# The last block's expert rows stay on chip and are added by a one-hot product, with the row loads no longer waiting for that block

## The reference, cut to what matters

```python
def step(acc, blk):
    e, tok, wt = blk
    xb = h[tok]
    hb = jax.nn.silu(xb @ we_g[e]) * (xb @ we_u[e])
    return acc.at[tok].add(wt[:, None] * (hb @ we_d[e]).astype(jnp.float32)), None
...
shared = (jax.nn.silu(h @ ws_g) * (h @ ws_u)) @ ws_d
return (routed + shared.astype(jnp.float32)).astype(h.dtype)
...
x = x + gt2 * rms_norm(yf, g_ffn_post)
```

## Time and profile before

| | |
|---|---|
| median of 3 runs | 1137.02 us (1135.15 to 1137.31) |
| the profiled execution's span | 1136.7 us |
| PE busy | 1096.6 us, 96% |
| DVE, ACT, POOL busy | 462.9, 236.6, 137.3 us |
| TensorE clock granted, mean of the span | 0.993 of full speed |
| DMA | 337.17 MB, mean 297 GB/s |

### The profile page before, as it was taken

The page is one execution under the profiler, slowest core; times in us unless marked ns, Lnnn a source line. Parts: engine busy times, 40 slices in busy tenths (PEclk is TensorE's granted clock), DMA queues, the critical chain, the costliest instruction groups (busy, mean ns, idle before and its releaser), DMA issues.

```text
span 1136.7 us, 16992 instructions
## 1 busy us (share of the span) xinstructions
PE 1096.6 (96%) x6443; PEld 576.4 (51%) x6443; DVE 462.9 (41%) x1286; ACT 236.6 (21%) x516; POOL 137.3 (12%) x163
## 2 busy tenths in 40 slices
PE   6999999999999999999989999999999999999896
PEld 3456677777877545754433443443343444343232
DVE  2218541665456645842264223223233232231157
ACT  4131241222233123111101111111111111111111
POOL 0110000000020110121111112111112111121100
PEclk9999999999999999999999999999999999999999
DMA  9978742042270372899999999999999999999898
GB/s 317 308 262 297 227 79 54 21 84 56 65 260 2 138 267 82 343 354 340 414 414 400 421 406 421 419 403 385 417 409 353 418 408 385 415 398 363 311 406 342
DMA packets 80743, 337.17 MB, mean 297 GB/s; under 512 B 10756, under 2 KB 27496, under 8 KB 52366
## 3 DMA queue, kind: packets, MB, share of 16 engines
q1 hardware_dynamic: 62606, 287.32, 66.4%
q0 software_dynamic: 18048, 48.68, 11.7%
HBM read 311.30 MB, written 37.24 MB: 307 GB/s over the span
## 4 chain that ended last, share of the span: by engine, by line
PE 87%; DMA 8%; DVE 2%; ACT 1%; issue 1%; SPq 1%; DVEq 0%; POOLq 0%; ACTq 0%
PE bank L1545 27%; PE bank L1568 15%; PE bank L1241 10%; PE bank L1260 5%; DMA mem<-in_w_exp_down 4%; PE bank L1533 3%; DMA mem<-expert_out_rows 3%; PE bank L1359 3%; PE bank L1360 3%; PE bank L1154 3%; PE bank L1477 3%; PE bank L1238 3%; PE bank L1129 1%; PE bank L1556 1%; PE bank L1324 1%
## 5 line engine op out<-in xcount | busy, mean ns | idle before, releaser
L1545 PE MATMUL bank<-mem 128*32 128x512 f32 (+2 forms) x1424 | 304.5, 594 | 2.6 <-issue 1.6
L1545 PEld LDWEIGHTS bank<-mem 128*32 128x32 f32 (+2 forms) x1424 | 100.2, 126 | 159.3 <-issue 157.9
L1568 PE MATMUL bank<-mem 128*32 128x512 f32 (+2 forms) x712 | 158.6, 599 | 5.1 <-DMA mem<-in_w_exp_down 5.1
L2231 DVE COPY mem<-bank 128x512 f32<-128x512 f32 x48 | 33.2, 692 | 292.2 <-PE bank L1533 292.2
L1545 PE MATMUL bank<-x_sb,mem 128*32 128x512 f32 (+2 forms) x480 | 141.6, 594 | 1.1 <-issue 1.1
L1241 PE MATMUL bank<-hT,mem 128*128 128x288 f32 x512 | 133.3, 409 | 1.0 <-ACT mem L919 1.0
L1241 PEld LDWEIGHTS bank<-hT,mem 128*128 128x128 f32 x512 | 93.8, 190 | 25.8 <-issue 2.4
L1049 ACT ACTIVATE mem<-bank 128x256 f32<-128x256 f32 x48 | 18.5, 385 | 316.7 <-PE bank L1556 316.5
L1568 PEld LDWEIGHTS bank<-mem 128*32 128x32 f32 (+2 forms) x712 | 49.1, 126 | 63.8 <-issue 60.3
L1568 PE MATMUL bank<-hT,mem 128*32 128x512 f32 (+2 forms) x240 | 72.8, 596 | 1.1 <-ACT mem L1049 1.1
L1545 PEld LDWEIGHTS bank<-x_sb,mem 128*32 128x32 f32 (+2 forms) x480 | 43.6, 127 | 59.1 <-issue 59.1
(11 more groups left out here) (403 smaller groups left out, 1290.4 us busy)
## 6 DMA issues: line engine op xcount, KB each, us to landing
mem<-in_w_exp_gate SPq DMA_DIRECT2D x48, 1024.0 KB
mem<-in_w_exp_up SPq DMA_DIRECT2D x48, 1024.0 KB
mem<-in_w_exp_down SPq DMA_DIRECT2D x48, 1024.0 KB
mem<-in_w_ada SPq DMA_DIRECT2D x8, 2048.0 KB, 9.8
x_sb<-in_w_exp_gate SPq DMA_DIRECT2D x16, 1024.0 KB
x_sb<-in_w_exp_up SPq DMA_DIRECT2D x16, 1024.0 KB
hT<-in_w_exp_down SPq DMA_DIRECT2D x16, 1024.0 KB
mem<-in_w_in SPq DMA_DIRECT2D x7, 2048.0 KB, 14.2
```

The lines of the kernel that those rows point to most:

```text
L1545: i = mm(bank[sl, :].rearrange("p (m f) -> p m f", m=2), xT[:, j % 2, c * BLK + sl.start:c * BLK + sl.stop], wview(r)[0][:, :, c, :], star ...
L1568: i = mm(ps[4 + hf][sl, :], hhT[:, k * BLK + sl.start:k * BLK + sl.stop], wview(r)[1][:, k, hf * 512:(hf + 1) * 512], start=k == 0, stop=k ...
```

## The change

The output of block 47 is no longer put into `yo` and scattered. ACT and DVE copy it into a buffer of its own, `ylast`. When block 45 is worked on, DVE makes from the token numbers of block 47's rows (`toklast`) a matrix `spot` of 128 rows by T tokens with a one where the row belongs to the token (`last_spots`). After the shared expert's products PE multiplies `spot` by `ylast` into the same PSUM banks (`last_down`), two products of 512 columns for each of the five tiles. Into the rows of `expert_out_rows` that block 47 would have written, POOL scatters zeros (`zrow`), before the scatter of block 46. SP waits for the zeros and block 46's scatter, no longer for block 47, then loads q = 0 to 3; before q = 4 it waits for block 47's products and then loads the x rows too. The slots of `yhalf` are numbered anew, since q = 0 and 1 share slot 0 and the next two lie over slots that block 47 doesn't use. In the last turn of the loop PE puts `down(46)` after three chunks of `up(47)`, and ACT and DVE copy block 46's output before they turn to `silu(47)` and `gated(47)`. The renamed semaphores are left out here.

```diff
@@ -303,6 +304,8 @@
         bcG, e_ = carve(mem, e_, [2, D])
+        zrow, e_ = carve(mem, e_, [D])
+        spot, e_ = carve(mem, e_, [T])
         at += NT * D
@@ -339,6 +342,7 @@
         yo, at = carve(hflat, 0, [2, D])
+        ylast, _ = carve(hflat, at, [D])
         dnX, at = carve(hflat, at, [FJ, D])
@@ -427,9 +431,13 @@
-        def ycount(q):
-            return 16 * (q // NYH + 1)
+        def yslot(q):
+            return 0 if q < 2 else (q - 1) % NYH
+        def yrows_sem(q):
+            return S[f"yb{yslot(q)}"], 16 if q <= NYH + 1 else 32
@@ -626,12 +634,10 @@
                     load_dn(r, ids.pop(r))
-            sp.wait_ge(S["eup"], max(LASTB[r] for r in range(NE) if slot(r) == XSLOT) + 1)
-            sp.wait_ge(S["xgT_t"], NBK)
-            for t in range(NT):
-                sp.dma_start(x_sb[0:ROWS[t], t, :], x1_d[t * P:t * P + ROWS[t], :]).then_inc(S[f"ld_x{t}"], 16)
             nov = overflow_count(sp)
-            sp.wait_ge(S["edn"], NBK)
+            def last_block():
+                sp.wait_ge(S["edn"], NBK)
@@ -647,33 +653,43 @@
-            overflow(sp, nov, body, last=last_rows)
-            sp.wait_ge(S["xgT_a"], NBK)
-            sp.wait_ge(S["xgT_d"], NBK)
+            overflow(sp, nov, body, last_block, last_rows)
             for k in range(2):
...
+            def x1_load(t):
+                sp.dma_start(x_sb[0:ROWS[t], t, :], x1_d[t * P:t * P + ROWS[t], :]).then_inc(S[f"ld_x{t}"], 16)
...
                 at_ = (k0 - q % 2 * KPE) * D
-                sp.dma_start(yhalf[0:ROWS[t], q % NYH, at_:at_ + (k1 - k0) * D], yv[t * P:t * P + ROWS[t], k0 * D:k1 * D]).then_inc(S[s], 16)
+                sp.dma_start(yhalf[0:ROWS[t], yslot(q), at_:at_ + (k1 - k0) * D], yv[t * P:t * P + ROWS[t], k0 * D:k1 * D]).then_inc(s, 16)
             for k in range(2):
-                sp.dma_start(yhalf[k:P:2, 0, :], yv[SEQ:T, KPE * k * D:KPE * (k + 1) * D]).then_inc(S[f"yh{k}"], 16)
+                sp.dma_start(yhalf[k:P:2, 0, :], yv[SEQ:T, KPE * k * D:KPE * (k + 1) * D]).then_inc(S[f"ys{k}"], 16)
             for i, (t, _) in enumerate(COMBINE):
...
                     q = 2 * i + k
-                    if q == NYH:
+                    if q == 4:
+                        sp.wait_ge(S["xgT_a"], NBK)
+                        sp.wait_ge(S["xgT_d"], NBK)
+                        sp.wait_ge(S["eup"], NBK)
+                        sp.wait_ge(S["edn"], NBK)
+                        for u in range(NT):
+                            x1_load(COMBINE[u][0])
+                    if q == 6:
                         sp.wait_ge(S["yd_sum"], 1)
-                    elif q > NYH + 1:
+                    elif q > 6:
                         sp.wait_ge(S["yd_sum" if (q - NYH) % 2 else "yp_mm"], (q - NYH) // 2 + 1)
                     if i < LAST:
-                        y_rows(q, t, k * KPE, (k + 1) * KPE, f"yh{q % NYH}")
+                        y_rows(q, t, k * KPE, (k + 1) * KPE, yrows_sem(q)[0])
                     elif k == 0:
-                        y_rows(q, t, 0, KPE // 2, "yh7")
-                        y_rows(q, t, KPE // 2, KPE, f"yh{q % NYH}")
-            y_rows(2 * LAST + 1, t, KPE, TOPK - 2, f"yh{(2 * LAST + 1) % NYH}")
-            y_rows(2 * LAST + 1, t, TOPK - 2, TOPK - 1, "yh5")
-            y_rows(2 * LAST + 1, t, TOPK - 1, TOPK, "yh6")
+                        y_rows(q, t, 0, KPE // 2, S["y8a"])
+                        y_rows(q, t, KPE // 2, KPE, yrows_sem(q)[0])
+                    else:
+                        y_rows(q, t, KPE, TOPK - 2, yrows_sem(q)[0])
+                        y_rows(q, t, TOPK - 2, TOPK - 1, S["ys0"])
+                        y_rows(q, t, TOPK - 1, TOPK, S["ys1"])
             for i, (t, _) in enumerate(COMBINE):
@@ -764,9 +780,10 @@
             pool.memset(xg2, 0.0).then_inc(S["pch"], 1)
+            pool.memset(zrow, 0.0).then_inc(S["pch"], 1)
             pool.wait_ge(S["st_x"], 16 * NT)
             pool.memset(xg3, 0.0).then_inc(S["pch"], 1)
-            pool.wait_ge(S["pch"], 2)
+            pool.wait_ge(S["pch"], 3)
             pool.wait_ge(S["h2_st0"], 16 * ((NT + 1) // 2))
@@ -802,9 +819,12 @@
                     ahead(b + XG, (b + XG) % RQ, gbuf(b + XG, b + XG))
+                if b == NBK - 1:
+                    q = (NBK - 1) % RQ
+                    pool.indirect_dma_start(y_d[:, :], bass.IndirectOffsetOnAxis(idxs[:, q:q + 1], 0), zrow, None,
+                                            bounds_check=T * TOPK - 1, oob_is_err=False).then_inc(S[f"sct{q % 2}"], 16)
                 if b >= 1:
                     scatter(b - 1, (b - 1) % RQ)
-            scatter(NBK - 1, (NBK - 1) % RQ)
             nov = overflow_count(pool)
@@ -1050,6 +1070,9 @@
                 act.wait_ge(S["edn"], n + 1)
+                if isinstance(n, int) and n == NBK - 1:
+                    a(ylast[:, 0:512], ps[4][:, :], ACT.Copy).then_inc(S["eout_a"], 1)
+                    return
                 if not (isinstance(n, int) and n < 2):
@@ -1604,18 +1629,20 @@
                 new_gu(b)
-                if b < NBK - 1:
-                    up(b, b, pieces(b))
-                else:
-                    up(b, b, pieces(b), range(KC - 2))
+                if b == NBK - 1:
+                    up(b, b, pieces(b), range(2))
+                    hh_T(b - 1)
+                    up(b, b, pieces(b), range(2, 3))
+                    new_dn(b - 1)
+                    down(b - 1, pieces(b - 1))
+                    up(b, b, pieces(b), range(3, KC))
+                    break
+                up(b, b, pieces(b))
                 if b == 0:
...
                     hh_T(b - 1)
-                if b == NBK - 1:
-                    up(b, b, pieces(b), range(KC - 2, KC))
-                if b < NBK - 1:
-                    x_T(b + 1, b + 1)
+                x_T(b + 1, b + 1)
                 if b + XG < NBK:
@@ -1658,8 +1685,18 @@
+            def last_down(o):
+                t, kp = COMBINE[o]
+                n = ROWS[t]
+                if o == 0:
+                    pe.wait_ge(S["srt_ready"], 2)
+                for hf in range(2):
+                    mm(ps[2 * (o % 4) + hf][0:n, :], spot[:, t * P:t * P + n], ylast[:, hf * 512:(hf + 1) * 512], start=False, stop=False)
...
                 shared_down(o)
+            for o in range(4):
+                last_down(o)
             pe.wait_ge(S["yd_sum"], 1)
@@ -1668,24 +1705,26 @@
                 if o < LAST:
-                    pe.wait_ge(S[f"yh{q % NYH}"], ycount(q))
+                    pe.wait_ge(*yrows_sem(q))
                 else:
-                    pe.wait_ge(S["yh7"], 16)
+                    pe.wait_ge(S["y8a"], 16)
                 for hf in range(2):
...
                         i = mm(ps[2 * (o % 4) + hf][0:n, :], ident[0:n, 0:n],
...
+                if o == LAST - 1:
+                    last_down(LAST)
@@ -2222,9 +2261,18 @@
                 o = ps[6]
+                if isinstance(n, int) and n == NBK - 1:
+                    step(ts(toklast[:, :], o[:, 0:1], o[:, 3:4], float(OOB), ALU.add, ALU.add))
                 ts(idxg[:, q:q + 1], o[:, 0:1], o[:, 3:4], float(OOB), ALU.add, ALU.add)
...
+            def last_spots():
+                for t in range(NT):
+                    n = ROWS[t]
+                    i = ts(spot[:, t * P:t * P + n], iota[:, 0:n], float(t * P), toklast[:, 0:1], ALU.add, ALU.is_equal)
+                i.then_inc(S["srt_ready"], 1)
@@ -2270,17 +2321,22 @@
                     xT_evac(b + 1, b + 1)
+                else:
+                    out_rows(b - 1, b - 1)
                 gated(b, b)
...
                     table(b - 6)
-                if b >= 1:
+                if b == NBK - 3:
+                    last_spots()
+                if 1 <= b < NBK - 1:
                     out_rows(b - 1, b - 1)
...
             def first_blocks():
+                dve.wait_ge(S["sct1"], 16 * (NBK // 2))
                 place_more(NBK, NBK, 0)
```

More of the change, by code:

```diff
@@ L180, in build @@
         ntab = sb("ntab", [P, 1], I32)
+        toklast = sb("toklast", [P, 1])
         negoff, at = carve(cst["cos"], 0, [NO])
@@ L355, in build @@
             P_ready idx_mm idx_ready gat0 gat1 gat2 xgT_t xgT_a xgT_d eup egs ehh ehT_t ehT edn eout_a eout_d sct0 sct1
-            ld_gu0 ld_gu1 ld_gu2 ld_gu3 ld_d0 ld_d1 ld_d2 ld_d3 srt_ready srt_mm over yp_mm yh0 yh1 yh2 yh3 yh4 yh5 yh6 yh7 yd_sum yl_sum yf_rt x2_done out_st dch ach pch pool_step""".split()
+            ld_gu0 ld_gu1 ld_gu2 ld_gu3 ld_d0 ld_d1 ld_d2 ld_d3 srt_ready srt_mm over yp_mm ys0 ys1 yb0 yb1 yb2 yb3 yb4 y8a yd_sum yl_sum yf_rt x2_done out_st dch ach pch pool_step""".split()
         S = {n: sem(n) for n in names}
@@ L1676, in _ @@
                         i = mm(ps[2 * (o % 4) + hf][0:n, :], ident[0:n, 0:n],
-                               yhalf[0:n, q % NYH, k * D + hf * 512:k * D + (hf + 1) * 512], start=False, stop=o < LAST and k == kp - 1)
```

(20 more changed lines are left out.)

6 lines of the change are left out of this document (3 added, 3 removed).

## The result

| | before | changed |
|---|---|---|
| median | 1137.16 us (1135.15 to 1137.72, 4 runs) | 1148.57 us (1147.32 to 1149.94, 4 runs) |
| span of the traced execution | 1136.7 us | 1145.5 us |
| ratio | | 1.0107, 95% interval 1.0094 to 1.0119 |

The changed kernel is 11.4 us slower. The prediction had the direction, but its time was 4.7 us too low, and the result lies above its range. Time and span of the same execution are known for the changed kernel: 1147.32 and 1145.5 us, so 1.8 us lie outside the span. So the two traces differ by only 8.8 us, and stretches are compared here, not spans.

A forecast was written before the change was run, and what follows sets the result against it. PE was taken as the bound, nearly as late as the transfers: + 2.8 start + 8.6 products - 4.8 waits + 0.3 clock = + 6.9 us, span 1143.6, time 1143.9 us; 8-in-10 range 1140.5 to 1147.3.

The forecast's parts named there:

- Later start of block 47: PE in block 47: down(47) starts at 1072.8 in place of 1070.01, 2.8 us later; without the weights' wait 0.9.
- Products: PE in the combination: ten float32 last_down products, 20 records of 0.43 us, add 8.6 us that no pause covers.
- Waits for rows: PE in the combination: its waits for expert rows vanish, giving back at most 4.77 us.
- The pause: PE behind block 47: the jump over the extra blocks' code stays, 6.4 us from down(47) to a combination starting at 1079.2.
- Clock: PE at the combination's start: a first stretch at half clock costs 1.7 us in place of 1.44, 0.3 more.
- More half-clock stretches: Rival: new pauses before down(46) and down(47) bring half clock, 1.7 us per stretch; 1145.6 to 1147.3 us, chance 0.18.
- The sum: PE's last product: + 2.8 + 8.6 - 4.8 + 0.3 = + 6.9 us, at 1136.5 in place of 1129.6.
- DVE goes along: DVE's sample-tile sum comes 9.7 us later than 1093.90; DVE and PE both reach the end at 1136.4 to 1136.5.
- Transfers: Row loads start at about 1072.5 (up to 1077), not 1079.67; the stream has 8 us to spare, so PE binds.
- Zeros, memset, `spot`: Small additions on transfers, POOL and DVE: zeros could delay down weights 0 to 1.2 us, taken as 0; the rest falls in waits.

The follow-up runs named there:

- run 7: The kernel before with only the new order in the last turn of the block loop on PE, ACT and DVE: 1139.17 us, ratio 1.0018.
- run 2: The changed kernel without the ten one-hot products (last block's rows left out of the result): 1139.72 us, 7.9 less than the changed kernel.
- run 3: The changed kernel with the first row load held until TensorE is through the first tile of shared_down: 1145.92 us, ratio 1.0083.
- run 4: The changed kernel with the old order in the last turn on TensorE, ACT and DVE: 1140.53 us, ratio 1.0043.
- run 6: The kernel before without the five x row loads during block 47 (final outputs left wrong): 1135.34 us, ratio 0.9989.
- run 8: The changed kernel with the old last-turn order and each f32 one-hot product done as two bf16 products: 1140.16 us, ratio 1.0032.
- run 5: The changed kernel with the old last-turn order and the first row load held back, as well: 1142.43 us, ratio 1.0049.
- run 9: The changed kernel with old last-turn order and bf16 product pairs, x loads spread over q = 5, 6 and 7: 1141.31 us, ratio 1.0036.
- run 10: The changed kernel with old last-turn order and bf16 product pairs, x loads back in block 47 ahead of all rows: 1137.93 us, ratio 1.0008.
- run 11: The changed kernel with old last-turn order and f32 products, x loads back in block 47 ahead of all rows: 1140.77 us, ratio 1.0038.
- run 1: The changed kernel measured again, unaltered: 1147.63 us, ratio 1.0097.

## Why the prediction was wrong

**Later start of block 47: right.** From the first product of `up(47)` to that of `down(47)` were 12.49 us and are 15.22 now (1056.00 to 1071.22): + 2.73, predicted + 2.8. The wait for block 46's weights was 1.79 us, predicted 1.9. Alone in the kernel before (run 7) the order costs 2.1 us net.

**Products: right.** 1096.39 to 1103.60 and 1129.59 to 1131.31, 8.9 us, predicted 8.6. Run 2 gives 7.9 in time.

**Waits for rows: right.** None is left, 4.77 us given back. Runs 3, 4, 6 and 8 show the other side: what TensorE saves returns as a wait. The stream had room in the changed kernel only because TensorE was so late.

**The pause: here it failed.** The step reads: "The pause that follows, a jump over the extra blocks' code, stays." It was taken as a cost of the jump alone, 6.4 us from the first product of `down(47)` to the combination. The first part nearly held (6.7 us), but a second pause of 2.63 us came on top, and in the same kernel's other trace the first part was 7.6. How long TensorE stands is not a matter of the jump alone but of what the DMA engines do beside it. In the quiet runs 3, 4, 5, 6, 8 and 9 the branch took 3.4 to 3.7 us and was over when `down(47)` was (within 0.2 us, in run 3 well before), and TensorE then waited 1.19 us for a copy. Beside the x loads (before, and runs 7, 10, 11) it took 5.6 to 8.1 us and the pause was 2.62 to 4.96. Beside the row loads of the changed kernel it took 6.1 to 7.2 us, and a second pause came behind it: 3.02 + 2.63, 3.95 + 0.89, 4.09 + 2.73. The shortest and the longest branch are those of runs 4 and 7:

```profile
L488 PEldq COMPARE_BRANCH  x1: 3426/3426/3426, 1067.8 to 1067.8; - x1
L480 PEldq COMPARE_BRANCH  x1: 8051/8051/8051, 1071.3 to 1071.3; - x1
```

The prediction named the row loads' new start (1072.5, where its own terms give 1072.0; it was 1069.78) and did not ask what else is on those DMA engines at that moment. The queue was in view: the page counts instruction queues (queue, packets, MB, share of 16 engines).

```profile
q8 instruction: 54, 0.88, 0.3%
q14 instruction: 35, 0.29, 0.1%
```

Their times fit. The packets of q8, 16 KB each, near the jump start at 1073.21, 1076.64 and 1080.47 us before, and at 1075.04, 1080.54 and 1086.87 us in the changed kernel. Against the branch, the thirteen traces fall into two groups. In the six quiet ones the first packet starts 1.0 to 1.3 us after the branch does; in the seven others it starts 2.7 to 5.3 us after. In all thirteen the branch ends 2.3 to 2.9 us after that packet starts. So all that the branch takes longer lies before the packet. The second packet starts 0.7 to 1.3 us after the branch ends in ten traces. In the three whose row loads were issued before the branch (the changed kernel twice, and run 2) it comes 3.2, 3.7 and 4.4 us after, and those are the three with a second pause. In them TensorE goes on 2.2 to 2.3 us after the second packet starts. (The distance to the third packet says nothing: it was over 6 us in runs 4, 7, 8, 9, 10 and 11 as well, without a second pause.)

That loads under way lengthen the pause is shown by runs 3 and 6. That it is by holding up these packets, and that q8 carries TensorE's code, is read from their times in all traces; no run moved the packets alone. The Trainium skill (DMA: Bandwidth & Descriptors, in Queues, rings and completion order) says that an engine takes turns between its queues packet by packet. By that rule a code packet waits for the row packet in hand on the same engine. The traces agree in the direction and not in the size: a packet of the rows took 0.61 us in the median and 1.6 at most over 1070 to 1090 us, and the first code packet was 2.7 us later than in the quiet runs. What makes up the rest is open.

**Clock: a size too small.** 0.3 us for it held in the shown trace (3.4 us at half clock, as before). But the same kernel again had 10.2 us of it in the traced execution, from 1077.1 on (0.56 over 1076 to 1086, run 1): some 4.2 us lost in place of 1.7, since TensorE stood still for 1.8 us of it. "More half-clock stretches" was a rival with 0.18, at + 1.7 to + 3.4; it was looked for in block 47, and in these traces came behind it (in run 3 it was in block 47). How much of it an execution has differs. Whether that is why those of the changed kernel spread over 2.6 us is not shown: their mean clocks are 0.997, 0.994, 0.991 and 0.992, and the last belongs to 1147.44 us, one of the two short ones.

**The sum.** From the start of `up(47)` to the end of the span were 79.2 us and are 89.5, + 10.3. The terms: 2.73 + 0.30 (first pause) + 2.63 (second) + 0.27 (clock) + 8.9 - 4.77 = 10.1. The prediction had 6.9; 2.9 of the 3.4 missing are the pauses, and 2.63 of them the second one, a term that the prediction did not have. What is left to the 11.4 us of the medians lies between executions: this trace is the fastest of the changed kernel's.

**DVE goes along: right.** The sample tile's sum moved from 1093.90 to 1105.63, + 11.7. The forecast was 9.7; with 2.9 us of pauses more, and 1.5 less by which this trace was ahead before block 47, it would be 11.1. Both reach the end together, DVE's last own sum and TensorE's last product at 1138.3 us:

```profile
1137.13 1.22 DVE L2382 TENSOR_TENSOR hT<-hT,mem 128x1024 f32<-128x1024 f32 x1
1138.45 1.28 DVE L2391 TENSOR_TENSOR hT<-hT,bank 128x512 f32<-128x512 f32 x2
```

**Transfers: right in what mattered.** The last row was there at 1130.8 us and not waited for. But it had been put at 1126 at best: the loads began 2.7 us earlier than reckoned and took 61 us, where 53 were reckoned, so that 5.7 us were to spare and not 8. That the stream alone would bind a faster TensorE was in the numbers, since 8 us to spare were less than the 8.6 of the products, but was not spelled out; runs 8 and 9 show it.

**Zeros, memset, `spot`: nothing measurable**, as taken. `down(46)` waited for its weights 1.66 us without the zeros (run 7) and 1.65 to 1.79 us with them (runs 2 and 3, the changed kernel). The blocks ahead were even 1.5 us earlier in the changed kernel's trace. That lead was 0.9 us by 400 us, 5.5 by 590, with the half-clock stretch of the earlier trace rows a part of it, and 1.3 again by 800; what makes it is not known, and it is taken as a difference between executions.

## What to carry to other kernels

Before moving a large load to an earlier time, list what else uses the DMA engines then, and the code of the engines belongs on that list wherever one jumps far: here TensorE's jump took 3.4 to 3.7 us alone and was hidden but for 1.19 us of waiting for a copy; with loads beside it TensorE stood up to 6.8 us (4.09 + 2.73). The branch instruction has a row of its own, which is to be read too, since the timeline puts its time down to "issue". A wait for a transfer is worth no more than the distance to the next bound: TensorE waited 4.77 us, and 8.9 us of TensorE work is a bad price for it. Where two resources end together, as rows and TensorE here, a gain on one shows up as a wait for the other, and only a change that relieves both is worth making.

## What the runs showed of the hardware

- TensorE's jump over a large branch: the branch instruction took 3.4 to 3.7 us without loads and with loads that only begin when it ends (runs 3, 4, 5, 6, 8, 9), 5.6 to 8.1 us with x loads under way, and 6.1 to 7.2 us with row loads at 410 GB/s under way. In the last case a pause of 0.9 to 2.7 us followed some records later. On DVE and ACT the same branch took 0.07 and 0.05 us.
- DVE pauses behind its branch, too, but not by the same rule: 4.63 to 5.16 us in the changed kernel and run 2, 4.63 in run 9, 2.18 in run 3, yet 3.10 in run 6, without loads, and 1.72 in run 10, beside the x loads. Why is open. Run 3 (DVE's timeline):

```profile
1080.02 0.22 DVE L2360 TENSOR_TENSOR mem<-c_ident 128x64 f32<-128x64 f32 x1 [2.18 <-issue]
```

- Half clock (1.2 of 2.4 GHz) came during or behind pauses of 2.6 us and more after block 47, and behind the row waits of 2.72, 4.99 and 3.79 us (runs 5, 8, 9); it never came behind the pause of 1.19 us alone. There are two exceptions. After the first pause of the changed kernel, 3.02 us, the clock stayed full over 1076 to 1080 and fell behind the second one. In run 3 it fell at 1071.9, in `down(47)`, behind pauses of 1.12 and 0.63 us, which four other traces have without it. The stretches lasted 3.4, 6.8 or 10.2 us.
- Two bf16 products of 512 columns cost half of one f32 product: 3.75 against 7.28 us for sixteen records.
